# A split-precision feed-forward product: 512 moving columns into two partial sums, added on VectorE

## The reference

```python
for l in range(DEPTH_2):                     # 2 layers
    ...
    h = _rms_norm(x, mlp_norm[l])            # 256 x 1024
    x = x + jnp.square(jax.nn.relu(h @ w_ff1[l])) @ w_ff2[l]    # 1024 x 4096, 4096 x 1024
```

## Time and profile before

| | us |
|---|---|
| median of 3 runs | 1713.44 |
| the profiled execution, its own time | 1710.85 |
| its span in the trace | 1709.0 |
| TensorE matmul busy | 1638.6 (96%) |
| weight load busy (overlaps) | 1502.8 |
| GpSimd busy | 1196.7 (70%) |
| ScalarE busy | 925.0 (54%) |
| VectorE busy | 882.5 (52%) |

### The profile page before, as it was taken

How to read it: one execution, slowest core, us unless ns; L and a number is a source line. 1 busy time by engine, 2 the same in 40 slices (tenths; PEclk the granted TensorE clock), 3 DMA queues, 4 the chain that set the end, 5 groups by cost and what they waited for, 6 DMA issues and landing times.

```text
span 1709.0 us, 32062 instructions
## 1 busy us (share of the span) xinstructions
PE 1638.6 (96%) x12800; PEld 1502.8 (88%) x12800; DVE 882.5 (52%) x1817; ACT 925.0 (54%) x1553; POOL 1196.7 (70%) x500
## 2 busy tenths in 40 slices
PE   8988999999999999999999999998999998999997
PEld 7876999999999998888888888777999986789997
DVE  6988446992366667777611115876220168752101
ACT  6666655445444445555566655665553447655533
POOL 5552777888877777777888887125888762268885
PEclk9999999999999999999999999999999999999999
DMA  7431555565555555555566664513656644145663
GB/s 263 126 123 54 190 168 169 173 192 180 181 165 170 166 172 166 175 177 174 192 195 189 195 197 136 183 52 116 190 181 188 189 149 162 51 148 185 183 188 112
DMA packets 79891, 280.42 MB, mean 164 GB/s; under 512 B 8704, under 2 KB 9472, under 8 KB 79488
## 3 DMA queue, kind: packets, MB, share of 16 engines
q1 hardware_dynamic: 79744, 278.38, 52.3%
HBM read 277.30 MB, written 1.05 MB: 163 GB/s over the span
## 4 chain that ended last, share of the span: by engine, by line
PE 84%; DVE 6%; issue 4%; ACT 3%; POOL 2%; DMA 0%; POOLq 0%; DVEq 0%; SPq 0%; ACTq 0%
PE ps L2660 14%; PE ps L2028 13%; PE ps L2329 10%; PE ps L2638 7%; PE ps L2639 7%; PE ps L2643 7%; PE ps L2667 7%; PE ps L537 6%; POOL wl L199 2%; ACT wh L184 1%; PE ps L2624 1%; PE ps L2626 1%; PE ps L371 1%; PE ps L2152 1%; PE ps L2122 1%
## 5 line engine op out<-in xcount | busy, mean ns | idle before, releaser
L199 POOL TENSOR_TENSOR wl<-slots,wh 128x1024 fp32r<-128x1024 f32 x236 | 572.7, 2430 | 355.8 <-ACT wh L184 339.9
L2438 POOL TENSOR_TENSOR wl<-slots,wh 128x1024 fp32r<-128x1024 f32 x256 | 619.2, 2420 | 141.4 <-ACT wh L2376 139.3
L2376 ACT ACTIVATE wh<-slots 128x1024 fp32r<-128x1024 f32 x256 | 271.4, 1060 | 367.8 <-issue 237.1
L184 ACT ACTIVATE wh<-slots 128x1024 fp32r<-128x1024 f32 x236 | 249.6, 1060 | 259.7 <-PE ps L2329 105.5
L2638 PE MATMUL ps<-xh,wh 128*128 128x256 f32 x1024 | 253.7, 285 | 0.0
L2639 PE MATMUL ps<-xl,wh 128*128 128x256 f32 x1024 | 250.8, 283 | 0.0
L2639 PEld LDWEIGHTS ps<-xl,wh 128*128 128x128 f32 x1024 | 196.2, 192 | 0.0
L2638 PEld LDWEIGHTS ps<-xh,wh 128*128 128x128 f32 x1024 | 196.0, 191 | 0.1
L2660 PE MATMUL ps<-wh,xh 128*128 128x512 f32 x508 | 159.3, 395 | 0.0
L2660 PE MATMUL ps<-wh,xl 128*128 128x512 f32 x508 | 157.1, 390 | 0.0
L2537 DVE TENSOR_TENSOR small<-ps,small 128x512 f16<-128x512 f32 x128 | 87.7, 685 | 118.6 <-PE ps L2626 118.6
(11 more groups left out here) (386 smaller groups left out, 3067.5 us busy)
## 6 DMA issues: line engine op xcount, KB each, us to landing
slots<-w SPq DMA_DIRECT2D x260, 512.0 KB, 3.6
slots<-wu SPq DMA_DIRECT2D x128, 512.0 KB, 3.6
slots<-wv SPq DMA_DIRECT2D x128, 512.0 KB, 3.5
arena<-bias SPq DMA_DIRECT2D x1, 2048.0 KB, 8.1
h<-xT SPq DMA_DIRECT2D x4, 256.0 KB, 5.6
arena<-keys SPq DMA_DIRECT2D x1, 1024.0 KB, 8.2
yT<-y_out SPq DMA_DIRECT2D x2, 512.0 KB, 2.7
layer<-consts SPq DMA_DIRECT2D x1, 800.0 KB, 5.3
```

The lines of the kernel that those rows point to most:

```text
L184: act.activation(self.hi[:, n % 2, :], self.slots[:, u % SLOTS, :], ACT.Copy).then_inc(self.rounded, 1)
L199: pool.tensor_tensor(self.lo[:, n % 2, :], self.slots[:, self.order[n] % SLOTS, :], self.hi[:, n % 2, :].bitcast(F32), ALU.subtract).then_ ...
L2376: act.activation(whv[:, r % 2, :], slots_v[:, r % SLOTS, :], ACT.Copy).then_inc(w_hi, 1)
L2438: pool.tensor_tensor(wlv[:, r % 2, :], slots_v[:, r % SLOTS, :], whv[:, r % 2, :].bitcast(F32), ALU.subtract).then_inc(w_lo, 1)
```

## The change

In pairs 2 to 15 of FF1, of both layers, each unit gets a bank of its own and is done by 8 matmuls of 512 moving columns (high weights by the high and the low activation side by side) and 8 of 256 columns (low weights by the high activation). Columns 0 to 255 then hold the sum with the high activation, 256 to 511 the one with the low activation. ScalarE copies the second half of each of the two banks to SBUF (`keep_second`), VectorE adds it: for the first unit in place, for the second unit from its own bank (`f_second`) into columns 256 to 511 of the pair's bank (`add_halves`). The 28 jobs of a layer go round banks 0 to 6. Each unit has its own entry in the ring, so unit n is released by its bank's full semaphore. On VectorE the order in the loop becomes `hidden_low(i-1)`, `add_halves(i)`, `relu(i)`, for pairs 0 and 1 too. `xh` and `xl` become halves of one tensor at the same place.

```diff
-        xh, xl = sb("xh", DC * T, F32R), sb("xl", DC * T, F32R)
+        both = sb("x_parts", 2 * DC * T, F32R)
+        xh, xl = both[:, 0:DC * T], both[:, DC * T:2 * DC * T]
+        x_parts = both[:, :].rearrange("p (k c t) -> p k c t", k=2, t=T)
...
+        l_half, l_both = sem("second_half_kept"), sem("halves_added")
+        second_half = lview(5888, 2, T)
...
             banks.plan([("f", l, 0), ("f", l, 1), ("mf", l)], mid3)
             banks.turn = 0
-            banks.plan([("f", l, i) for i in range(2, 6)], low4)
-            banks.turn = 0
-            banks.plan([("f", l, i) for i in range(6, 16)], mid3)
+            banks.plan([(n, l, i) for i in range(2, 16) for n in ("f", "f_second")], seven)
...
-                      + pairs_of([("f", l, i) for i in range(16)]) + [None] * 31 + [("f2", l, 3)], True)
+                      + pairs_of([("f", l, i) for i in range(2)])
+                      + [(n, l, i) for i in range(2, 16) for n in ("f", "f_second")] + [None] * 31 + [("f2", l, 3)], True)
...
+                def keep_second(i, j):                       # ScalarE
+                    b = banks.take(act, (("f", "f_second")[j], l, i))
+                    if j == 0 and 14 * l + i > 2:
+                        act.wait_ge(l_both, 14 * l + i - 2)
+                    elif j == 1 and i > 2:
+                        banks.wait_drained(act, ("f_second", l, i - 1))
+                    act.activation(second_half[:, j, :], b[:, T:2 * T], ACT.Copy).then_inc(l_half, 1)
+
                 for i in range(1, 16):
                     ring.round(act, 1)
                     if i == 3:
...
                         hidden(3)
                     elif i > 4:
                         hidden(i - 1)
+                    if i >= 2:
+                        keep_second(i, 0)
                     ring.round(act, 1)
+                    if i >= 2:
+                        keep_second(i, 1)
                 hidden(15)
...
+                def add_halves(i):                           # VectorE
+                    b = banks.take(dve, ("f", l, i))
+                    dve.wait_ge(l_half, 28 * l + 2 * (i - 2) + 1)
+                    dve.tensor_tensor(b[:, 0:T], b[:, 0:T], second_half[:, 0, :], ALU.add).then_inc(l_both, 1)
+                    other = banks.take(dve, ("f_second", l, i))
+                    dve.wait_ge(l_half, 28 * l + 2 * (i - 2) + 2)
+                    banks.give(dve.tensor_tensor(b[:, T:2 * T], other[:, 0:T], second_half[:, 1, :], ALU.add),
+                               ("f_second", l, i))
+                    dve.wait_ge(l_both, 14 * l + i - 1)
+                    banks.wait_drained(dve, ("f_second", l, i))
+
                 for i in range(17):
+                    if i:
+                        hidden_low(i - 1)
+                    if 2 <= i < 16:
+                        add_halves(i)
                     if i < 16:
                         relu(i)
-                    if i:
-                        hidden_low(i - 1)
...
+                def wide_unit(job):                          # TensorE
+                    bank = banks.open(pe, job)
+                    w = ring.high(pe).rearrange("p (k n) -> p k n", k=DC)
+                    for k in range(DC):
+                        pe.matmul(two(bank[:, :]), w[:, k, :], x_parts[:, :, k, :], start=(k == 0), stop=False,
+                                  skip_group_check=True)
+                    w = ring.low(pe).rearrange("p (k n) -> p k n", k=DC)
+                    for k in range(DC):
+                        ins = pe.matmul(bank[:, 0:T], w[:, k, :], xhT[:, k, :], start=False, stop=(k == DC - 1),
+                                        skip_group_check=True)
+                    banks.close(ins, job)
+
                 for i in range(16):
+                    if i >= 2:
+                        wide_unit(("f", l, i))
+                        wide_unit(("f_second", l, i))
+                        continue
                     split_pair(("f", l, i), 2 * l + 1 if i == 0 else None)
```

More of the change, by code:

```diff
@@ L294, in build @@
         arena = memory.enter_context(nc.sbuf_tensor("arena", [P, ARENA], F32))
-        xhT, xlT = (x[:, :].rearrange("p (c t) -> p c t", t=T) for x in (xh, xl))
+        xhT, xlT = (x.rearrange("p (c t) -> p c t", t=T) for x in (xh, xl))
         whv, wlv = (x[:, :].rearrange("p (b n) -> p b n", b=2) for x in (wh, wl))
```

## The result

The changed kernel takes 1719.06 us (median of 10 runs, 1716.41 to 1722.43) against 1714.01 us before (10 runs beside them, 1713.22 to 1716.38): a ratio of 1.0028, 95% interval 1.0018 to 1.0038. It is slower, by 5.05 us; 4.8 was forecast.

The account below looks back on a forecast made before the run. TensorE's stream was taken to bound the kernel. Per layer, stops 4.15 + 0.5 and restarts 0.6 less gain 2.87 give +2.4, twice +4.8 on 1713.44: 1718.2 us, forecast's own range 1715.5 to 1720.5, 8 in 10 1713.0 to 1722.8.

Parts of the forecast that it names:

- The steady state: Mid FF1: TensorE alone sets the pace at 2.77 us a unit instead of 2.88; other engines keep slack of 0.8 and 1.0.
- 8 matmuls of 512 take 1.81 us: FF1's wide matmuls: 226.6 ns each, taken from another stage of the trace, against 240 for two of 256.
- The gain: TensorE in FF1: 28 units x 0.107 = 2.98 us per layer at most, 2.87 after the 0.11 lost in unit 4.
- The bound of 240 ns: Rival for FF1's wide matmuls: a 512 of two runs costs 240 ns, no gain, 1722.4 us; chance 0.10.
- A start price for unit 4: FF1's unit 4: its third product already waits 0.24 for GpSimd; a shorter first part waits longer, losing 0.11 us.
- The start of FF1: Units 8, 9 and 11: VectorE's and ScalarE's order stalls TensorE, 4.15 us per layer plus five restarts of 0.1.
- the restarts: TensorE's first group after a stop takes 1.06 instead of 0.96; each stop costs 0.1 us more, 0.6 per layer.
- FF2's first bank: Start of FF2: all four banks open at once and bank 3 is held by pair 14; stall 0.5 and 0.1 to restart.
- The second layer: FF1 of the second layer has the same length to 0.01 us, so the +2.4 per layer counts twice: +4.8.
- The other side: Rival: the saving shows and FF1's start does not stall, only bank 3's stall stays; 1708.9 us, chance 0.16.
- The free time named for that side: Support for the no-stall rival at FF1's start: GpSimd and ScalarE have a quarter to a half of their time free.
- The clock: Rival: the clock falls with the stops, +3.3 us for both layers, 1721.5 us; chance 0.02.

Follow-up runs that it names:

- experiment 8: Changed kernel with the narrow products made wide too, by added low by low products, so all matmuls of a unit have 512 columns; 1757.02 us, timed once.
- Experiment 1: Changed kernel with only ScalarE's order made even, hidden(i-1) at every i, none bunched at i = 3 and 4; 1710.25 us against 1713.84 before, ratio 0.9977.
- 3: Kernel before, 256-column products kept, with only VectorE's new order, hidden_low(i-1) ahead of relu(i); 1714.53 us, timed once.
- 4: Changed kernel with relu(1) put ahead of hidden_low(0) on VectorE, all else as changed; 1717.01 us, timed once.
- Experiment 2: Changed kernel with FF2 opening each output bank right ahead of its first product there, not all four at once; 1722.37 us, timed once.
- 5: Changed kernel with 8 unused floats ahead of x_parts, so x_parts, wh and wl start at a multiple of 64 bytes; 1718.46 us, timed once.
- experiment 7: Changed kernel with each chunk's high and low part side by side, so a wide matmul's moving operand is one run of 512; 1717.71 us, timed once.
- the even order: Changed kernel with ScalarE's hidden(i-1) at every i; alone 1710.25 us, with FF2's banks opened one by one 1709.23, with moved operands too 1708.92.
- experiment 6: Kernel before with 8 unused floats allocated ahead of xh, moving the operands by 32 bytes; 1714.78 us against 1713.21, ratio 1.0008.
- experiment 9: Kernel before with consecutive FF1 matmuls, all pairs but pair 0, writing the bank's two halves in turn; 1714.14 us, timed once.

## Why the prediction was right

It held in the time (1718.2 forecast, 1719.06 measured), in the sign, and in the mechanism of the steady state and of the stops; two terms were off in size, and that the second layer is as the first did not hold quite.

- *The steady state.* TensorE alone sets the pace from unit 12 on, as said. The unit was forecast at 2.77 and is 2.79. The term that was mis-sized is "8 matmuls of 512 take 1.81 us": it came from a stage where all matmuls are wide, and a change of width costs 0.02 net per unit, 0.55 us per layer (experiment 8). The gain is 28 x 0.087 = 2.4 instead of 2.98. The bound of 240 ns was not near.
- *A start price for unit 4.* 0.29 in the row, forecast 0.24 plus what the shorter part leaves; right in kind.
- *The start of FF1.* Forecast stops 0.5, 1.6, 0.6, 0.85, 0.6. The distances between matmuls around them, less those of the stream, are 0.50, 1.60, 0.46, 0.84 and 0.46, the restarts on top. Where and for whom is as forecast, down to ScalarE's two waits for VectorE. Experiment 1 showed that none of it comes without ScalarE's bunched order, 3 that VectorE's order has a part of 1.0 even without the sums, 4 that relu(1) put ahead again gives back 1.35.
- *FF2's first bank.* Forecast 0.5 and 0.1, measured 0.8. `hidden_low(14)` ended at 1278.83 + 0.69 = 1279.52, and the first matmul came at 1279.89, 0.37 later, where behind a wait for GpSimd it took 0.04. The trace file also holds TensorE's wait instructions, which the views above leave out. Behind the end of `hidden_low(14)` there are three, at 1279.56 (line 106, bank 3), 1279.67 (line 213, the rounded weights) and 1279.78 (line 126, pair 0), with the waits for the other banks among them and on the weight load at 1279.86. What the second and third wait for had come more than 1 us before, but each takes its turn, 0.11 apart. At unit 8 the one wait is on the weight load itself, and 0.05 passed. So the wait for the bank was 0.5 as forecast (the stream was due at 1278.13 + 0.95 = 1279.08), and the mis-sized term is the restart. Experiment 2 removes it with the wait.
- *The second layer.* It was taken as the first. It is 0.37 longer: unit 11 waits 1.04 for its rounding instead of 0.68, because `relu(3)` starts 0.46 late for no wait that the profile shows:

```profile
1552.52 0.70 DVE L2000 SCALAR_TENSOR_TENSOR ps<-ps,rst 128x512 f32<-128x512 f32 x1 [0.46 <-issue]
```

  The same difference of 0.35 to 0.37 is in experiments 2, 4, 5 and 7, and in none with the even order. Its cause is open.
- *Sum.* Per layer (first): stops and restarts 5.1, gain 2.35, +2.75; forecast 5.25 - 2.87 = +2.4. The short gain (0.5) and FF2's stop (0.2) err one way, GpSimd's two stops (0.3) the other. Both layers together are 5.9 us longer where 4.8 was forecast. That the medians lie only 0.3 from the forecast's difference is in part luck: their interval, 0.0018 to 0.0038 of 1714, is 3.1 to 6.5 us and holds both.
- *Rivals.* The other side, at 1708.9 with only FF2's stop left, is what experiment 1 built by changing ScalarE's order: 1710.25. Its condition, unit 9's rounding before 1205.3, it misses by 2.2 us: 1211.54, less the 4.06 by which its stage starts later, is 1207.5, as forecast (1207.55). The free time named for that side was misread: the earlier trace rows has GpSimd busy for 57.74 of 69 us, so 16% of its time is free, not a quarter; ScalarE's 42% is within what was said. The clock stayed at 1.00 through all stops of the stage: the window over the changed kernel's stage, stops, seven banks in turn and all, has 1.00 in the clock's column (the other columns as in the earlier trace rows), and so has the second layer's.

```profile
1200.00:1280.00 80.00, 76.31 (x431) 65.90 (x431) 30.27 (x56) 52.51 (x85) 65.26 (x28) 1.00 0.56 183
```

  TensorE stood still for 80.00 - 76.31 = 3.7 us of it.

## What to carry to other kernels

When a change adds work that is well hidden in the steady state, walk through the first rounds of the loop, engine by engine: here a hand-written order with two catch-up steps lost 4 us a layer at the start where the loop itself gained 2.4. ScalarE's added waits of 1.43 and 1.23 us were waits for all that stood behind them in its order of work, the next weights' rounding among it, and TensorE stopped 1.44 us for that; so look at what is queued behind a wait, not at how busy the engine is (ScalarE 55%). The bank plan that goes round seven banks tied one of its last jobs to the next stage's first matmul, 0.8 us a layer (experiment 2); open each bank where it is first written. And count the waits that stand behind the one that ends last: 0.05 us passed at unit 8, 0.37 where three wait instructions had to be gone through.

## What was not expected of the hardware

- Merging two 256-column matmuls with one stationary operand into one of 512 gains 13.3 ns (2 x 120.0 - 226.6; in experiment 8 too the wide ones are 226 or 227 apart), in a stream where every matmul has its own weight load. With narrow groups between, as in the changed kernel, 87 / 8 = 10.9 ns are left.
- Eight wide matmuls between narrow ones take 1.84 us instead of 1.81: the first five are 228 to 236 ns apart, the rest 226 to 227; the narrow ones behind start with 113 and 119.
- A moving operand of two runs of 256 costs the same as one of 512 (1.84 us for eight, experiment 7), and its start moved by 32 bytes (by the sizes of the tensors allocated ahead, from 32 bytes past a multiple of 64 to the multiple) makes no difference to TensorE (81.30 against 81.27 us of stage, 1.0008 in time). GpSimd's subtractions took some 0.02 us longer with it (2.42 us in the mean before, 2.44 in experiment 6).
- FF2's matmuls of 256 columns follow each other at 117.8 ns in the mean, FF1's at 120, and the place of the sums is not why (still 120 in experiment 9).
- TensorE's three wait instructions ahead of FF2 start 0.11 us apart, though what the second and third wait for has long come (1279.56, 1279.67, 1279.78; in the second layer 1615.62, 1615.73, 1615.83).
